# A hybrid diffusion block on one core: end with tokens on partitions, first projection input made inside attention, two modulation vectors made by VectorE

## The reference, cut to what matters

```python
sh_m, sc_m, gt_m, sh_f, sc_f, gt_f = split(silu(c) @ ada_w + ada_b)      # 0 .. 5
h = rmsnorm(x, g_mix_pre) * (1 + sc_m) + sh_m
y = concat(hyena(h), neighbourhood_attention(h), rg_lru(h)) @ w_out      # 256 + 512 + 256 -> 1024
x = x + gt_m * rmsnorm(y, g_mix_post)                                    # gt_m is vector 2
h = rmsnorm(x, g_ffn_pre) * (1 + sc_f) + sh_f
x = x + gt_f * rmsnorm((silu(h @ w_g) * (h @ w_u)) @ w_down, g_ffn_post) # gt_f is vector 5
```

## Time and profile before

| | |
|---|---|
| median of 3 runs | 1521.18 us (1519.98 to 1521.59) |
| the profiled execution, its own time | 1515.61 us |
| its span in the profile | 1513.8 us |
| TensorE matmul, weight load | 94%, 76% of the span busy |
| VectorE, ScalarE, GpSimd | 50%, 36%, 41% |
| mean DMA rate over the span | 103 GB/s |
| shares of the chain that ended last | TensorE 77%, VectorE 9%, ScalarE 3% |

### The profile page before, as it was taken

The page is one execution under the profiler, slowest core; times in us unless marked ns, Lnnn a source line. Parts: engine busy times, 40 slices in busy tenths (PEclk is TensorE's granted clock), DMA queues, the critical chain, the costliest instruction groups (busy, mean ns, idle before and its releaser), DMA issues.

```text
span 1513.8 us, 20444 instructions
## 1 busy us (share of the span) xinstructions
PE 1418.0 (94%) x7699; PEld 1156.4 (76%) x7699; DVE 753.7 (50%) x1039; ACT 540.1 (36%) x845; POOL 614.0 (41%) x282
## 2 busy tenths in 40 slices
PE   5899999899997999899999999999999999999994
PEld 1588667889986877678778888878878888878883
DVE  6675449873927788437976112133455212121235
ACT  4672652222215776544332222222222222221220
POOL 2462113531327452274334444444533444444540
PEclk9999999999999999999999999999999999999996
DMA  9852003114104443432323333323334333332321
GB/s 332 281 187 77 28 28 112 42 42 139 42 15 124 127 127 113 153 94 87 125 81 88 96 97 97 97 87 100 91 93 130 97 97 97 97 94 84 97 87 56
DMA packets 236955, 156.57 MB, mean 103 GB/s; under 512 B 11043, under 2 KB 222385, under 8 KB 236763
## 3 DMA queue, kind: packets, MB, share of 16 engines
q1 hardware_dynamic: 234899, 148.71, 32.4%
q10 hardware_dynamic: 1992, 6.99, 1.3%
HBM read 147.25 MB, written 8.81 MB: 103 GB/s over the span
## 4 chain that ended last, share of the span: by engine, by line
PE 77%; DVE 9%; ACT 3%; SPq 3%; POOL 3%; DMA 2%; issue 2%; ACTq 0%; DVEq 0%
PE ps L1823 32%; PE ps L1828 16%; PE ps L1984 10%; PE ps L1987 5%; PE ps L2140 2%; PE ps L2106 1%; POOL w_lo L1090 1%; PE ps L2117 1%; PE ps L2000 1%; SPq L511 1%; DVE pr L1651 1%; DMA rpad<-zpad 1%; PE ps L2041 1%; PE ps L2029 1%; PE ps L2120 1%
## 5 line engine op out<-in xcount | busy, mean ns | idle before, releaser
L1074 POOL TENSOR_TENSOR w_lo<-raw,w_hi 128x1024 fp32r<-128x1024 f32 x152 | 372.8, 2453 | 459.0 <-ACT w_hi L685 459.0
L1823 PE MATMUL ps<-hb_hi,w_hi 128*128 128x512 f32 x832 | 329.6, 396 | 16.0 <-ACT w_hi L685 5.8
L1823 PE MATMUL ps<-hb_lo,w_hi 128*128 128x512 f32 x832 | 327.4, 393 | 0.0
L685 ACT ACTIVATE w_hi<-raw 128x1024 fp32r<-128x1024 f32 x152 | 160.0, 1053 | 187.6 <-PE ps L1828 179.3
L1828 PE MATMUL ps<-hb_hi,w_lo 128*128 128x512 f32 x832 | 209.9, 395 | 1.9 <-POOL w_lo L1074 1.9
L1823 PEld LDWEIGHTS ps<-hb_hi,w_hi 128*128 128x128 f32 x832 | 158.3, 190 | 53.3 <-DVE hb_lo L1701 7.6
L1090 POOL TENSOR_TENSOR w_lo<-raw,w_hi 128x1024 fp32r<-128x1024 f32 x22 | 97.1, 4417 | 224.2 <-ACT w_hi L841 224.2
L1828 PEld LDWEIGHTS ps<-hb_hi,w_lo 128*128 128x128 f32 x832 | 157.8, 190 | 37.6 <-issue 2.5
L1823 PEld LDWEIGHTS ps<-hb_lo,w_hi 128*128 128x128 f32 x832 | 158.4, 190 | 32.6
L1984 PE MATMUL ps<-ha_hi,w_hi 128*128 128x512 f32 (+2 forms) x432 | 163.6, 379 | 3.7 <-ACT w_hi L841 3.3
L1984 PE MATMUL ps<-ha_lo,w_hi 128*128 128x512 f32 (+2 forms) x432 | 160.9, 372 | 0.0
(11 more groups left out here) (252 smaller groups left out, 2047.7 us busy)
## 6 DMA issues: line engine op xcount, KB each, us to landing
raw<-in_ffn_w_gu SPq DMA_DIRECT2D x88, 512.0 KB, 3.8
ada1x<-in_ada_w SPq DMA_DIRECT2D x32, 512.0 KB, 3.9
raw<-in_ffn_w_down SPq DMA_DIRECT2D x32, 512.0 KB, 3.9
raw<-in_w_in SPq DMA_DIRECT2D x22, 512.0 KB, 3.9
ada<-in_ada_w SPq DMA_DIRECT2D x4, 2048.0 KB, 21.7
raw<-in_w_out SPq DMA_DIRECT2D x16, 512.0 KB, 4.0
raw<-in_ffn_w_down SPq DMA_DIRECT2D x16, 384.0 KB, 3.5
raw<-in_ktab SPq DMA_DIRECT2D x8, 512.0 KB, 6.0
```

What stands on the lines that cost most here:

```text
L685: act.activation(w_hi[:, b, :], raw[:, b, :], ACT.Copy).then_inc(hi_done, 1)
L1074: pool.tensor_tensor(w_lo[:, b, :], raw[:, b, :], w_hi[:, b, :].bitcast(F32), ALU.subtract).then_inc(lo_done, 1)
L1823: pe.matmul(dst, w_hi[:, b, k * P:(k + 1) * P], x, start=start and k == 0 and n == 0, stop=False)
```

## The change

It does four things.

1. **Modulation.** Only chunks of the vectors 3 and 4 (`ADA0` = 24, `ADAN` = 16) are still made inside attention, in blocks 0 to 15. Vectors 2 and 5 are made elsewhere: eight whole row blocks of 128x1024 (`rows_dma`, 512 KB each) are scaled by a per-partition number and added up by VectorE (`modulation_rows`, one operation of 128x1024 for each block), and TensorE sums over partitions by eight matmuls of one column. For vector 2 this lies in the first half of the output projection, for vector 5 in the gate and up tiles 7 to 14 of half 0.
2. **First projection input.** ScalarE splits seven of the eight input tiles of half 0 (`mix_head`) in steps 25 to 31 of the attention loop, and the first two `w_out` tiles (`head_of`) in steps 29 and 30; GpSimd makes the low parts; SP loads the two `w_out` tiles when the scores of head pair 2 are done. Only tile 5 is split after the last block (by ScalarE, then VectorE), and the first job takes the tiles in the order `EARLY` + (5,). TensorE waits for `mx_ok` 64 instead of `ot_free` 32 and `modp`. The four `x` loads (`xr2`) and two `rows_dma` now stand before the load of the third `w_out` tile.
3. **The end.** The residual `x1` of half 1 is transposed early, in the down jobs of half 1 (`x1_columns`, 32 transposes), and every down tile is squared by ScalarE, scaled by `gffn` on the copy out of PSUM and transposed four times (`down_columns`, 32 transposes, the last four after the last job). With tokens on partitions the variance is 128x4 numbers, and after the reciprocal there are two VectorE operations of 128x512 and one store for each of four token tiles.
4. VectorE copies four banks (`yta`) midway, since the transposed tiles need eight banks and have four.

```diff
+EARLY = (0, 1, 6, 7, 2, 3, 4)
+ADA0, ADAN = 24, 16
...
+            def rows_dma(dst, m, c, n):
+                sp.wait_ge(mod_rd, 16 + n - 1)
+                sp.dma_start(dst[c % 2][:], ada[:, c, m * D:(m + 1) * D]).then_inc(ada_ld[c % 2], 16)
...
+                if n == 26:
+                    sp.wait_ge(qk_done, 24)
+                    pair0(J_OUT, src_o)
+                if n < ADAN:
+                    chunk_dma(n)
             sp.wait_ge(pv_done, 32)
-            pair0(J_OUT, src_o)
             for q in range(4):
                 sp.dma_start(xr2[0][:, q, :], x_tok[q * P:(q + 1) * P, :]).then_inc(xr_ld, 16)
-            phase(J_OUT, 4, src_o)
+            for c in range(2):
+                rows_dma(adq, 2, c, ADAN + c)
+            for i in range(1, 4):
+                for b in range(2):
+                    raw_dma(b, J_OUT + 2 * i + b, src_o(i, b))
+                for c in (2 * i, 2 * i + 1):
+                    rows_dma(adq, 2, c, ADAN + c)
...
+                if 25 <= n < 32:
+                    mix_head(EARLY[n - 25])
+                if n in (29, 30):
+                    act.wait_ge(t_ok, 48)
+                    head_of(J_OUT + n - 29)
...
+            for i, k in enumerate(EARLY):
+                pool.wait_ge(m_hi, i + 1)
+                pool.tensor_tensor(hm_lo[k][:], mix_src(k, 0), hm_hi[k][:].bitcast(F32), ALU.subtract).then_inc(m_lo, 1)
+                if i == 4:
+                    rest_of(J_OUT)
...
             for k in range(KT):
+                for c in range(2 * k, min(2 * k + 2, KT)):
+                    modulation_rows(adq, adq_sum, c, ADAN // 2 + c // 2 + 1)
                 dve.wait_ge(acc_free, E_OUT + k + 3)
                 add_square(yo[0][:, k, :], k, yacc, ysq)
...
-            pe.wait_ge(ot_free, 32)
-            pe.wait_ge(modp, 1)
+            pe.wait_ge(mx_ok, 64)
+            pe.wait_ge(modp, 2)
+            for m in range(KT):
+                pe.matmul(ps[:, 7, m:m + 1], adq_sum[:, m * P:(m + 1) * P], ones[:, 0:1], start=True, stop=True).then_inc(mod_done, 1)
...
+                    for k in range(KT):
+                        for c in range(3):
+                            down_job(k // 2, 3 * (k % 2) + c)
+                        if k == 0:
+                            x1_columns(2)
+                            x1_columns(3)
+                        else:
+                            down_columns(k - 1)
+                    down_columns(KT - 1)
+            pe.wait_ge(n_sum, 6)
+            for q in range(4):
+                ins = pe.matmul(ps[:, 0, q:q + 1], nrm[:, q * P:(q + 1) * P], ones[:, 0:1], start=True, stop=True)
...
+                        act.activation(sq[:, k % 2, :] if k else nrm[:], ps[:, 2 + k % 2, :], ACT.Square).then_inc(y_sq, 1)
+                        act.activation(ydg[:, k % 2, :], ps[:, 2 + k % 2, :], ACT.Copy, scale=gffn[:, k:k + 1]).then_inc(dn_free, 1)
...
+            link(dve.reciprocal(rstd4[:], var4[:]))
+            for q in range(4):
+                dve.scalar_tensor_tensor(ost[:, q, 0:HALF], yta[:, q, :], rstd4[:, q:q + 1], x1t[:, q, 0:HALF], ALU.mult, ALU.add)
+                dve.scalar_tensor_tensor(ost[:, q, HALF:D], ps[:, 4 + q, :], rstd4[:, q:q + 1], x1t[:, q, HALF:D],
+                                         ALU.mult, ALU.add).then_inc(o_ev, 1)
```

More of the change, by code:

```diff
@@ L307, in program @@
         hbias = small("hbias", [8])
+        var4 = small("var4", [4])
+        rstd4 = small("rstd4", [4])
         amin = small("amin", [2, 2])
@@ L651, in _ @@
                 if h == 0:
-                    phase(J0, FT, src_g)
+                    for i in range(1, 15):
+                        for b in range(2):
+                            raw_dma(b, J0 + 2 * i + b, src_g(i, b))
+                        if i == 2:
+                            sp.wait_ge(job_done, J_FFN)
+                        for c in (range(2) if i == 2 else (i - 7,) if i >= 9 else ()):
+                            rows_dma(adf, 5, c, ADAN + 8 + c)
+                    phase(J0, FT, src_g, 15)
                 else:
@@ L1173, in mix_rests @@
                     pool.tensor_tensor(lo[:, k, :], mix_src(k, h), hi[:, k, :].bitcast(F32), ALU.subtract).then_inc(m_lo, 1)
-            mix_rests(0, range(5, 8), hb_hi, hb_lo)
-            rest_of(J_OUT)
-            for j in range(1, 16):
+            pool.wait_ge(qk_done, 24)
+            pool.wait_ge(t_ok, 48)
+            for i, k in enumerate(EARLY):
[3 more added lines that the diff above has]
+                    rest_of(J_OUT)
+            rest_of(J_OUT + 1)
+            for j in range(2, 16):
                 rest_of(J_OUT + j)
@@ L1769, in _ @@
                     gu_tile(6)
+                    for c in range(KT):
+                        gu_tile(7 + c)
+                        modulation_rows(adf, adf_sum, c, ADAN // 2 + 4 + c // 2 + 1)
+                    dve.nop().then_inc(modp, 1)
                 else:
@@ L1814, in _, with product @@
         @block.tensor
         def _(pe):
-            def product(J, b, dst, rhs, nk=KT, start=True, stop=True, between=None, ready=None):
+            def product(J, b, dst, rhs, nk=KT, start=True, stop=True, between=None, ready=None, order=None):
                 pe.wait_ge(hi_done, J + 1)
-                for k in range(nk):
+                for i_, k in enumerate(order or range(nk)):
                     if ready:
@@ L1822, in product @@
                     for n, x in enumerate(rhs(k)):
-                        pe.matmul(dst, w_hi[:, b, k * P:(k + 1) * P], x, start=start and k == 0 and n == 0, stop=False)
+                        pe.matmul(dst, w_hi[:, b, k * P:(k + 1) * P], x, start=start and i_ == 0 and n == 0, stop=False)
                 if between:
@@ L2133, in values @@
                     pe.wait_ge(ot_free, v)
-                pe.matmul(ps[:, 7, 384 + v:385 + v], arow1[:, b, :], selc[:, 0:1], start=True, stop=True).then_inc(mod_done, 1)
+                if v < ADAN:
+                    pe.matmul(ps[:, 7, 384 + v:385 + v], arow1[:, b, :], selc[:, 0:1], start=True, stop=True).then_inc(mod_done, 1)
                 for c in range(5):
@@ L2235, in _ @@
                 if h == 0:
+                    pe.wait_ge(modp, 3)
+                    for m in range(KT):
+                        pe.matmul(ps[:, 7, m:m + 1], adf_sum[:, m * P:(m + 1) * P], ones[:, 0:1], start=True, stop=True).then_inc(mod_done, 1)
                     sum_over_features(3, nrm)
@@ L2238, in _ @@
                 pe.wait_ge(g_al, FT * (h + 1))
-                with pe.Fori(0, 4) as i:
-                    for q in range(6):
-                        f, c = q // 3, q % 3
-                        nk = KT if c < 2 else FT - 2 * KT
-                        if c == 0:
-                            pe.wait_ge(dn_free, i * 2 + (8 * h + f + 1))
-                        product(i * 6 + (J0 + q), q % 2, ps[:, 2 + f, :],
-                                lambda k: (a_hi[:, c * KT + k, :], a_lo[:, c * KT + k, :]), nk, start=c == 0, stop=c == 2)
```

199 lines of the change are left out of this document (132 added, 67 removed).

## The result

The changed kernel takes **1506.45 us** in the median (1505.14 to 1508.21, four runs) against 1520.8, a gain of 14.3 us by the medians. The ratio of the two kernels' times is 0.9914, 95% interval 0.9897 to 0.9931, which is 13.1 us. The forecast was 1503.8, a gain of 17.4, and the time lies in the range. That one was among the fastest: the kernel before ran from 1515.1 to 1528.0 over all the runs of this study, the changed one from 1503.1 to 1513.1. So stages are compared by traces, and the whole by medians. One execution of a later run, of 4944.6 us, is left out everywhere.

A forecast was written before the change was run, and what follows sets the result against it. TensorE was taken to set the pace nearly everywhere, with three exceptions. Attention 5.0, seam 2.6, vector 5 0 and end 9.8 sum to 17.4 off the median of 1521.2: 1503.8 us, range 1496 to 1512.

The forecast's parts named there:

- the seam: From attention's last values into the output projection: 7.4 gained less 1.0, 0.6, 1.7 and 1.5, net 2.6 us; bounds -3 and 5.7.
- the end: After the last product: 13.7 us in place of 30.1, less 6.6 for 60 transposes among down jobs; net 9.8 saved.
- attention: Blocks 16 to 31 without chunks: 2.0 in pair 2, 2.0 in pair 3, 1.0 in the last turn; 5.0 us saved.
- the third rival: New company in head pair 3 and late loads: pair 3 gains 0, the seam -1, about 1509.5 us; chance 0.16.
- pair 3: Attention's blocks 24 to 31: 5.1 us saved, less 1.6 and 1.5 for new company, so 2.0.
- The tail, which was to gain 1.0: Attention's last turn and its copy shorten by 0.58 + 0.16 + 0.21, 1.0 us with rounding.
- ScalarE's and GpSimd's new work: In head pair 3: two `head_of` delay exponentials, 1.6 us; two `rest_of` reach into VectorE's scalings, 1.5 us.
- VectorE's chain in pair 2: Eight blocks of attention beside GpSimd's tables: 35.6 us against the 37.6 of before, so 2.0 saved.
- The wait for the third tile: Output projection: third `w_out` tile queued behind four `x` and two row loads, costing TensorE 1.0 us (0 to 4).
- GpSimd's backlog: Output projection: GpSimd runs behind and its start slips a little against TensorE; cost 0.6 us (0 to 2).
- the squares: VectorE's row operations and squares of tiles 3 to 7 delay the sum TensorE wants in job 8; cost 1.5 us (0 to 3).
- the fourth rival: TensorE's clock falls in attention, about 2.5 us more per block at half clock; up to 1544 us; chance 0.05.

The follow-up runs named there:

- the end alone: The kernel before with only the new end (changes 3 and 4 without 1 and 2): 1508.53 us, ratio 0.9916 to the kernel before.

## Why the prediction was right, and where it was not

**The total** came out 3.1 us short of the gain forecast, and hides a larger miss: by the traces the seam fell 7.7 short, while the end gave 2.0 and attention 0.6 more. (Those parts sum to 12.3, and 1.6 came at the start of half 1, where nothing was forecast; the medians say 14.3 and 14.4, within what single profiles scatter.) That the number still lies near the forecast is in part luck: errors of both signs met. It isn't the third rival, in which pair 3 gained nothing and the seam lost 1; but the late loads of that rival did come, and cost more than it said.

**Attention, 5.0: measured 5.6.** Pair 2 gained 1.6 in the one profile whose clock was 0.95, and 2.4 by the others (35.2), for 2.0, against a profile of before at full clock. Pair 3 with the tail gained 4.0 for 3.0, but not as split: the quiet block came to 3.58 in the mean (forecast 3.59) and blocks 24 to 30 gained 4.3, with no company to pay. The tail, which was to gain 1.0, lost 0.3: two `head_of` and two `rest_of` fall there. The 3.1 set against ScalarE's and GpSimd's new work was too much by some 1.6. The time worked out for VectorE's chain in pair 2 (35.6) held to 0.4. Here the Trainium skill, "SBUF — State Buffer", section "SBUF: two separate sides", gave the third rival: each new GpSimd operation could hold one scaling for its length. Its mechanism shows in the rows at 677 (0.69 becomes 2.77, ending just after GpSimd's 2.39) and at 615.23 (0.55 becomes 2.06). But of the nine operations only that one held a scaling up: five began during VectorE's maximum, which reads PSUM and kept its 0.72 to 0.82 us, one lay beside a scaling that kept its 0.55, and the last two came after the last scaling. So pair 3 kept its gain.

**Seam, 2.6: measured -5.1.** The gap and the clock of job 0 came back as said (5.84 + 1.44 for 7.4), and so did the one-column matmuls (job 7: 1.70 for 1.7). Three terms were right in kind and wrong in size. The wait for the third tile was put at 1.0; it was 3.8 to 3.9, and the low clock after it cost 2.75 in one profile and 1.7 in the other. The load landed about 13.7 us after the last values, against the 10.5 to 11 that I worked out with 414 GB/s, the rate of two microseconds in the trace before; from 626.24 to 640 the mean rate was 302. And I priced the wait but not the clock that a wait of that length brings, which the earlier trace rows showed (7.01 for 5.44 after 5.84 of idleness). GpSimd's backlog was put at 0.6 and cost 1.9 (jobs 5 and 6) in the first profile and 1.4 (jobs 4 to 6) in the second; the squares were put at 1.5 and cost 2.1 and 3.5 (job 8). These two I had costed by VectorE's own time, at quiet durations; a run without the row operations gives back 6.0. The bound for the seam was -3 (-3.3 by its own terms), and it was broken: the bound of 4 on the wait held in these two profiles (4.32 in a third), and the clock was in no bound.

**Vector 5, 0: measured 0.** 1.84 us of matmuls took the place of the wait of 2.05.

**The end, 9.8: measured 11.8 by the trace, 12.9 by the run of the end alone.** The tail took 11.95 for 13.7: 3.5 to the first of the eight VectorE operations (for 3.9), 5.4 for these, at a pace of 0.66 (for 6.0), and 3.1 from their end to the span's (for 3.8). The down products lost 6.3 for 6.6. The rule of the Trainium skill, "TensorE: Matmul & The Clock Gate", section "Part 4: PE-mode transpose", that speaks of about 275 ns for a transpose, agrees with the duration listed for each (273 ns) but not with the price, 0.11 in a row of four, eight or sixteen at full clock; and the clock stood at 1.00 from 1372 to the last product.

**The clock in attention**, the fourth rival: over head pair 3 the clock was 1.00, though TensorE was idle for 4.5 of 37.04 us, and over pair 2 it was 0.95 in one profile and 1.00 in the next, so it didn't come. Blocks 0 to 15, the same code in all but the chunks' contents, take 77.2 to 84.0 us, so they alone move a single execution by up to 7 us.

**What stays open:** why a pause of the same length, in the same place, is sometimes followed by half clock and sometimes not. In job 5 TensorE waits 1.88 in the kernel before, and its next eight matmuls take 2.11; with the end alone the same wait is followed by

```profile
672.84 3.12 PE L1863 MATMUL ps<-hb_hi,w_lo 128*128 128x512 f32 x8 [1.88 <-POOL w_lo L1099]
```

No run here decides that.

## What to carry to other kernels

Work taken from the engine that binds isn't free where it lands: seven operations of 1.3 us on an idle VectorE cost 6 us there, 4.1 of them because they held up GpSimd, on whose output the next products wait, and 1.5 because VectorE's own sum came late; cost moved work by what it does to its neighbours, and ask whether the loop that it leaves was bound by it at all. When a prefetch moves across a stage, order its queue by who needs the data first, price the load with the mean rate of the stretch and not the best one, and allow, for every wait of TensorE of some us, for a slow clock after it (0 to 2.75 us here). Take waits out together: removing the first of two in a row gave back a third of what it had cost.

## What the runs showed of the hardware

- Two row operations of 128x1024 with both inputs in SBUF took 1.28 each alone and 2.3 to 2.7 beside GpSimd's subtractions, whose 128x1024 took 2.39 alone and 2.9 to 3.4 there. I had expected the loser to be one side only.
- The same code in the same stretch ran at a mean clock of 1.00 or of 0.92, with equal waits (77.2 to 80.0 us for 16 blocks).
- After a wait of 2.5 for VectorE sixteen transposes took 2.62 in the first profile of the changed kernel (at 1365.84) and 3.33 in the second, and 1.91 at full clock.
- The same wait of 1.88, in the same job, was followed by eight matmuls of 2.11 in two profiles and of 3.12 in a third.
